# A 31-tap depthwise convolution as block-Toeplitz products, in the mixer of a decoder layer

## The chip, the cores and the metric

The kernel runs on one core of a Trainium2 chip, in one launch. The metric is the time on the device in microseconds (us), the median of the runs. Engines: TensorE (PE), VectorE (DVE), ScalarE (ACT), GpSimd (POOL) and SyncE (SP), which only issues DMAs here. Each runs its own queue of instructions in order; they meet at semaphores.

## The reference

One decoder layer on 1024 prompt tokens and 8 x 4 sample tokens: FFN 1, a mixer, FFN 2, and a gated embedding. The change is in the mixer's convolution head:

```python
h = rmsnorm(x, pre_g)
u = h @ w_in
u_val, u_glu, u_x, u_gelu = jnp.split(u, [D_CONV, 2 * D_CONV, 2 * D_CONV + D_LRU], axis=-1)
g = u_val * jax.nn.sigmoid(u_glu)
gp = jnp.concatenate([conv_buf, g], axis=1)          # 30 past rows in front
c = causal_dwconv(gp, conv_w, conv_b)                # 31 taps, each channel by itself
c = jax.nn.silu(rmsnorm(c, conv_norm_g))
new_conv_buf = gp[:, -(CONV_WIDTH - 1):, :]
```

D_CONV is 512 channels. The prompt has zeros in front, the eight sample sequences have a cache of 30 rows each. Beside it stands the RG-LRU head on u_x (a 4-tap convolution, two gates, a linear recurrence over time); both heads go through w_out.

## The kernel before

Features lie on the partitions, tokens along the free axis: 1056 tokens in three chunks c of C = 352, of which the last has 320 prompt and 32 sample tokens. Most matrices are fp32 split into a high and a low part in a rounded format, and each product is three passes (L589 to L591). `tile_product` is 8 x 3 such products with 352 columns. Weights come in units of 256 columns through one raw buffer: SP loads two halves (`load_wide`), ACT rounds them (`split_half`), DVE takes the rest (`split_tile`). A down weight of an FFN comes the same way through `rawd`: `load_down`, `split_down`.

Each FFN has NI = 11 steps; in a step PE forms gate and up tiles, then down tiles. The first and the last step are written out, nine are in a loop. SP has a loop of its own (`ffn_loads`), and after it load_down and two load_wide for the last step and the mixer. In the last step (`ffn_last`) the norms of the earlier chunks are done beside the products.

In the mixer, `vg_chunk` and `in_unit(2)`, `in_unit(3)` form u_val and u_glu for the four channel groups j of 128; DVE scales them by the norm and multiplies by the sigmoid, into `gp` (prompt, with 30 columns of history) and `gs` (samples). Then come twelve turns x. In a turn PE does the tile of u_x for one j and c, `conv_group` for another j and c, and `lru_gates` (six products into ps_aux). DVE does `lru_front` (scale, four taps, low part, with ACT's rounding `xc_hi` between), five of its own conv taps, and `lru_scan` of the turn before. ACT does sigmoids, exp, tanh, square root, with a table load (1.28 us) at each switch. lru_r, lru_i, lru_a and lru_q exist once, so the gates of turn x wait for the scan of turn x - 1, and xc exists twice.

The 31 taps are shared out: TP = 15 are products with a diagonal matrix on PE (fp32, not split), 16 are multiply-adds over all tokens on DVE (`conv_taps`), and `conv_join` adds both. ACT writes the diagonals (`diagonals`). `conv_states` carries the last 30 columns back to token order by PE transposes, for the new caches. After the turns follow gelu (units 6 and 7), the convolution's norm and silu, and w_out.

PSUM has a ring of six banks whose order is worked out ahead (`ring_plan`), and two more banks, ps_aux, in an order of their own (`aux_plan`). Each engine's order is written by hand.

Of the kernel before, what the change touches and what calls it, by code (L numbers as in the profile page):

```python
# [21 lines left out]
F32 = mybir.dt.float32  # L22
# [4 lines left out]
P = 128  # L27
# [3 lines left out]
NJ = 4  # L31
# [9 lines left out]
TP = 15  # L41
# [21 lines left out]
def ring_plan():  # L63
# [21 lines left out]
    for s in range(2):  # L85
        put("cache", s)
    for u in (2, 3):
        for c in range(NC):
            for t in range(2):
                put("in", u, c, t)  # L90
    for x in range(NJ * NC):
        put("in", 4 + x // 6, x % 6 // 2, x % 2)
        put("conv", x // NC, x % NC)
        if x == 0:
            for s in range(3):
                put("convout", s)
# [41 lines left out]

def aux_plan():
# [9 lines left out]
    for i in range(first):  # L149
        norm(i)  # L150
    for x in range(4 * NC):
        for which in "ri":
            at[which, x] = n
            n += 1
# [37 lines left out]
def build(nc, a, out):  # L192
    ctx = ExitStack()
    with ctx:
# [60 lines left out]
        y_lo, yl_at, _ = place("y_lo", [P, KT, TOK], F32R)  # L255
        gp, g_at, _ = place("gp", [P, NJ, CH + SEQ])
        mix_end = at[0]

        gs, _, e = place("gs", [P, NJ, NB, CH + DEC], offset=norm_at)
        assert e <= sq_at  # L260
        assert max(ffn_end, mix_end) <= nc.sbuf_usable_end, (ffn_end, mix_end, nc.sbuf_usable_end)
        row = 4 * TOK
        conv = place("conv", [P, NJ, TOK], offset=yl_at)[0]
        hs = place("hs", [P, NJ, TOK], offset=yl_at + 4 * row)[0]
        cache_in = place("cache_in", [P, 2, NJ * P], offset=yl_at + 4 * row)[0]
        gs_new = place("gs_new", [P, NJ, NB * CH], offset=yl_at + 4 * row)[0]
        gate_raw = place("gate_raw", [P, 2, NJ, P], offset=yl_at + 4 * row + 4096)[0]
        cv_stage = place("cv_stage", [P, 3, NJ * P], offset=yl_at + 6 * row)[0]
# [4 lines left out]
        diag, _, e = place("diag", [P, TP, P], offset=e)  # L273
        assert e <= yh_at + 4 * row
        gw_hi, _, e = place("gw_hi", [P, 2, NJ, P], F32R, offset=yh_at + 4 * row)
        gw_lo, _, e = place("gw_lo", [P, 2, NJ, P], F32R, offset=e)
        assert e <= yh_at + 6 * row
        xc = place("xc", [P, 2, C], offset=yh_at + 6 * row)[0]
        lru_r = place("lru_r", [P, C], offset=yh_at + 6 * row + 8 * C)[0]
        lru_i = place("lru_i", [P, C], offset=yh_at + 6 * row + 12 * C)[0]  # L280
        lru_a = place("lru_a", [P, C], offset=yh_at + 6 * row + 16 * C)[0]
        lru_q = place("lru_q", [P, C], offset=yh_at + 6 * row + 20 * C)[0]
        glu = place("glu", [P, 2, C], offset=yl_at + 6 * row)[0]
# [4 lines left out]
        assert e <= mix_end  # L288

# [28 lines left out]
        def conv_w(tap, j):  # L318
            n = P + tap * NJ + j
            return params[:, n:n + 1]  # L320
# [37 lines left out]
        cache_read = sem("cache_read")  # L358
# [4 lines left out]
        gs_new_done = sem("gs_new_done")  # L363
        conv_step = sem("conv_step")
        diag_done = sem("diag_done")
        diag_free = sem("diag_free")
# [78 lines left out]
        def _(sp_eng):  # L445
# [18 lines left out]
            def ffn_loads(f):  # L464
# [38 lines left out]
            eng.wait_ge(psum_full, RING["ffn", 0] + NI * STEP)  # L503
            for s in range(2):
                eng.dma_start(cache_in[0:4 * CH, s, :],
                              a["cache_conv"][0, 4 * s:4 * s + 4].rearrange("b w n -> (b w) n")
                              ).then_inc(cache_read, 16)
# [15 lines left out]
            for v in range(WIDE0["mix"] + 6, WIDE0["mix"] + 9):  # L523
                load_wide(v)
# [1717 lines left out]
```

## Time and profile before

| | us |
|---|---|
| median of 3 runs | 2345.52 |
| lowest, highest | 2345.4, 2349.55 |
| span of the profiled execution | 2337.7 |
| PE, DVE, ACT busy in it | 2158.0, 1317.6, 769.8 |

The span runs from the first to the last instruction; the runs' times hold in addition what lies around it, 7.8 us at the median. In rows of the profile, L589 is line 589 of the kernel, `out<-in` names tiles, `x24` counts instructions. In timelines the first column is the start, the second the length (of a merged row, from the first start to the last end); brackets give the idle time in front and who ended it. PE products overlap, so starts are compared, not lengths.

### The profile page before, as it was taken

To read this page: it belongs to the slowest core of one execution; us is meant where nothing else is said; L and a number is where in the kernel's file an instruction comes from. 1 tells how busy PE (TensorE), PEld (TensorE's weight loads), DVE (VectorE), ACT (ScalarE), POOL (GpSimd) and SP (SyncE) were. 2 spreads that over 40 slices of the span, in tenths; PEclk is the share of its full clock that TensorE was granted. 3 is DMA by queue.
4 is the path that set the end of the run, shared out by engine and by line. 5 is a ranking of instruction groups with operands and counts; after the bars stand their busy time and mean duration, and the time that the engine had idled before them with its cause. 6 is when DMAs were issued, how large, how long until landed. Compare 5 with 4: busy or idle time off the path is not lost. (4 is left out here: it accounts for less than half of the span.)

```text
span 2337.7 us, 34611 instructions
## 1 busy us (share of the span) xinstructions
PE 2158.0 (92%) x13020; PEld 2106.1 (90%) x13020; DVE 1317.6 (56%) x2620; ACT 769.8 (33%) x1500; POOL 0.9 (0%) x8
## 2 busy tenths in 40 slices
PE   5899999999999878999989689999999999995886
PEld 5899999999999878887789689999999999995886
DVE  4544444543445666988555764545434554557686
ACT  4311121221122333365575532212221121225563
POOL 0000000000000000000000000000000000000000
PEclk8999999999999889999999889999999999998897
DMA  4101111101111011100014201111101111102222
GB/s 149 37 28 45 54 54 54 54 27 35 45 54 54 1 45 41 46 1 19 19 38 144 91 1 55 55 54 54 45 18 45 54 54 54 54 1 73 72 91 75
DMA packets 92360, 116.15 MB, mean 50 GB/s; under 512 B 4596, under 2 KB 83704, under 8 KB 92282
## 3 DMA queue, kind: packets, MB, share of 16 engines
q1 hardware_dynamic: 91065, 110.79, 14.4%
q10 hardware_dynamic: 1216, 4.33, 0.6%
q8 instruction: 48, 0.79, 0.1%
q14 instruction: 31, 0.25, 0.0%
HBM read 110.15 MB, written 4.95 MB: 49 GB/s over the span
## 5 line engine op out<-in xcount | busy, mean ns | idle before, releaser
L589 PE MATMUL ps<-x_hi,w_lo 128*128 128x352 f32 x2688 | 883.2, 329 | 17.8 <-DVE w_lo L1503 8.8
L590 PE MATMUL ps<-x_lo,w_hi 128*128 128x352 f32 x2688 | 872.9, 325 | 0.0
L591 PE MATMUL ps<-x_hi,w_hi 128*128 128x352 f32 x2688 | 871.9, 324 | 0.0
L589 PEld LDWEIGHTS ps<-x_hi,w_lo 128*128 128x128 f32 x2688 | 514.6, 191 | 19.1 <-DVE w_lo L1503 9.5
L590 PEld LDWEIGHTS ps<-x_lo,w_hi 128*128 128x128 f32 x2688 | 515.3, 192 | 0.0
L591 PEld LDWEIGHTS ps<-x_hi,w_hi 128*128 128x128 f32 x2688 | 513.5, 191 | 0.0
L589 PE MATMUL ps<-a_hi,wd_lo 128*128 128x352 f32 x1104 | 361.6, 328 | 24.6 <-DVE a_lo L1600 11.6
L590 PE MATMUL ps<-a_lo,wd_hi 128*128 128x352 f32 x1104 | 357.7, 324 | 0.0
L591 PE MATMUL ps<-a_hi,wd_hi 128*128 128x352 f32 x1104 | 357.3, 324 | 0.0
L1650 DVE TENSOR_TENSOR acc<-ps,acc 128x352 f32<-128x352 f32 x480 | 249.3, 523 | 88.7 <-PE ps L591 82.8
L1583 DVE TENSOR_TENSOR tmp_u<-ps,rstd_pre 128x352 f32<-128x352 f32 x132 | 69.1, 524 | 370.7 <-PE ps L591 370.7
L1022 ACT ACTIVATE w_hi<-raw,params 128x256 fp32r<-128x256 f32 x512 | 213.6, 496 | 132.0 <-DMA raw<-in_ffn_w_gu_dram 109.1
L1503 DVE SCALAR_TENSOR_TENSOR w_lo<-raw,params,w_hi 128x256 fp32r<-128x256 f32 x512 | 225.8, 477 | 46.7 <-ACT w_hi L1022 46.7
L1089 ACT ACTIVATE tmp_s<-tmp_g 128x352 f32<-128x352 f32 x132 | 65.3, 498 | 552.1 <-DVE tmp_g L1583 552.1
L589 PEld LDWEIGHTS ps<-a_hi,wd_lo 128*128 128x128 f32 x1104 | 210.4, 191 | 27.6 <-DVE a_lo L1600 12.8
L590 PEld LDWEIGHTS ps<-a_lo,wd_hi 128*128 128x128 f32 x1104 | 210.9, 191 | 0.0
L591 PEld LDWEIGHTS ps<-a_hi,wd_hi 128*128 128x128 f32 x1104 | 210.1, 190 | 0.0
L1583 DVE TENSOR_TENSOR tmp_g<-ps,rstd_pre 128x352 f32<-128x352 f32 x132 | 68.5, 522 | 244.1 <-PE ps L591 230.0
L1098 ACT ACTIVATE a_hi<-tmp_a 128x352 fp32r<-128x352 f32 x132 | 59.9, 494 | 418.4 <-DVE tmp_a L1594 418.4
L829 PE MATMUL ps<-gp,diag 128*128 128x352 f32 (+1 forms) x360 | 108.8, 460 | 3.5 <-ACT diag L1284 3.5
L1526 DVE TENSOR_TENSOR ssum<-ssum,sq 128x352 f32<-128x352 f32 x177 | 92.6, 523 | 22.3 <-ACT sq L1048 9.5
L829 PEld LDWEIGHTS ps<-gp,diag 128*128 128x128 f32 x360 | 69.2, 194 | 38.1 <-issue 5.5
(172 smaller groups left out, 1678.2 us busy)
## 6 DMA issues: line engine op xcount, KB each, us to landing
raw<-in_ffn_w_gu_dram SPq DMA_DIRECT2D x88, 512.0 KB, 3.5
rawd<-in_ffn_w_down_dram SPq DMA_DIRECT2D x22, 1024.0 KB, 7.6
raw<-in_w_out_dram SPq DMA_DIRECT2D x24, 512.0 KB, 3.5
raw<-in_ple_w_gate_dram SPq DMA_DIRECT2D x24, 512.0 KB, 3.4
raw<-in_w_in_dram SPq DMA_DIRECT2D x16, 512.0 KB, 4.0
x_in<-in_x_prompt_dram ACTq DMA_DIRECT2D x6, 512.0 KB, 7.8
out_dram<-y_stage SPq DMA_DIRECT2D x6, 512.0 KB, 2.8
rawd<-in_ple_w_proj_dram SPq DMA_DIRECT2D x1, 1024.0 KB, 7.2
```

Source lines behind the costliest of these rows:

```text
L589: eng.matmul(dst, wl, xh, start=first, stop=False)
L590: eng.matmul(dst, wh, xl, start=False, stop=False)
L591: return eng.matmul(dst, wh, xh, start=False, stop=last)
L829: mm = eng.matmul(dst[:, 0:w], diag[:, tap, :], gp[:, j, at0:at0 + w], start=tap == 0, stop=tap == TP - 1)
L1022: ins = eng.activation(w_hi[s][:, sl], raw[:, sl], ACT.Copy, scale=vec(gain, k))
L1089: eng.activation(tmp_s[:, h, :], tmp_g[:, h, :], ACT.Silu).then_inc(silu_done, 1)
L1098: eng.activation(a_hi[:, h, cols(c)], tmp_a[:, h, :], ACT.Copy).then_inc(a_hi_done, 1)
L1503: ins = eng.scalar_tensor_tensor(w_lo[s][:, sl], raw[:, sl], vec(gain, k), f32(w_hi[s][:, sl]), ALU.mult, ALU.subtract)
L1526: eng.tensor_tensor(ssum[:, i % 2, :], ssum[:, i % 2, :], sq[:, (ADD0[i] + m - 1) % SQ, :], ALU.add).then_inc(add_done, 1)
L1583: eng.tensor_tensor((tmp_u if up else tmp_g)[:, h, :], src, rstd_pre[:, cols(c)], ALU.mult).then_inc(psum_free, 1)
L1650: eng.tensor_tensor(acc[:, m, cols(c)], src, acc[:, m, cols(c)], ALU.add).then_inc(psum_free, 1)
```

## The change

The convolution is written as products along time. Time is cut in blocks of BLK = 32. DVE transposes each 32x32 square of `gsrc` (channels x time, j odd and even in turn) into `gt_even` or `gt_odd`, so that a partition is a place in the block and each of four groups of 32 partitions holds 32 channels of its own. For one channel in each of the four groups at once (`cc`), a 128x128 matrix with four Toeplitz squares on its diagonal acts on 48 block columns (32 of the prompt, 16 for the samples); a second matrix does so on the block before. `conv_slot(t)` is that for CG = 8 values of cc: 16 full fp32 products. Sixteen slots t make up the four j. ACT copies a slot to `zt` (`conv_evict`), DVE transposes back (`to_channels`), and the bias is added later, inside the square and the scale.

The Toeplitz squares come from a table in DRAM. DVE lays the reversed taps in `rev` after step 0 of FFN 1; SP writes shifted rows of it to `toeplitz`, eight DMAs behind its loop in FFN 1; each slot loads its part with four DMAs (`load_toep`), alternately into two buffers. GpSimd clears the buffers and carries caches in and new caches out straight from gt. The twelve turns lose conv_group, conv_taps, conv_join and the diagonals; slots 0 to 7 stand between the tiles of units 2 and 3, slots 8 to 15 in turns 1 to 4.

```diff
+def conv_after(x):
+    return range(2 * CSLOT + 2 * (x - 1), 2 * CSLOT + 2 * x) if 1 <= x <= CSLOT else ()
...
+                if f == 0:
+                    eng.wait_ge(rev_done, 2)
+                    for j in range(NJ):
+                        for half in range(2):
+                            first = rev[:, j, 2 * BLK * half + BLK - 1:2 * BLK * half + BLK]
+                            rows = bass.AP(tensor=first.tensor, offset=first.offset,
+                                           ap=[first.ap[0], [-1, BLK], [1, BLK]])
+                            eng.dma_start(toep_dram[P * j:P * j + P, half, :, :], rows
+                                          ).then_inc(taps_out, 16)
                 load_down(d0 + NI - 1, down_src[f][NI - 1])
...
+            def load_toep(t):
+                if t < 2:
+                    eng.wait_ge(taps_out, 16 * 2 * NJ)
+                    eng.wait_ge(zero_done, (7, 5)[t])
+                else:
+                    eng.wait_ge(aux_full, AUX["conv", t - 2] + 1)
+                if t == 2 * CSLOT + 1:
+                    eng.wait_ge(zero_done, 8)
+                j, s = divmod(t, CSLOT)
+                for q in range(4):
+                    src = toep_dram[P * j + BLK * q + CG * s:P * j + BLK * q + CG * s + CG
+                                    ].rearrange("c h p n -> p (c h) n")
+                    eng.dma_start(toep(t)[BLK * q:BLK * q + BLK, :, :, BLK * q:BLK * q + BLK
+                                          ].rearrange("p cc b n -> p (cc b) n"), src
+                                  ).then_inc(toep_in[t % 2], 16)
...
+            def conv_slot(t):
+                j, s = divmod(t, CSLOT)
+                n = AUX["conv", t]
+                eng.wait_ge(aux_free, n - 1)
+                if s == 0:
+                    eng.wait_ge(gt_done, 2 * j + 2)
+                    eng.wait_ge(cache_in[j % 2], 64 * (j // 2 + 1))
+                eng.wait_ge(toep_in[t % 2], 64 * (t // 2 + 1))
+                for cc in range(CG):
+                    dst = ps_aux[:, n % 2, cc * NOUT:cc * NOUT + NOUT]
+                    for back in range(2):
+                        mm = eng.matmul(dst, toep(t)[:, cc, back, :],
+                                        gt(j)[:, 1 - back:1 - back + NOUT, CG * s + cc],
+                                        start=back == 0, stop=back == 1)
+                mm.then_inc(aux_full, 1)
+
+            in_unit(2, lambda k: k >= 2 and conv_slot(k - 2))
+            in_unit(3, lambda k: k < CSLOT and conv_slot(CSLOT + k))
...
-                conv_group(x // NC, x % NC)
+                for slot in conv_after(x):
+                    conv_slot(slot)
                 if x == 0:
-                    conv_states()
                     eng.wait_ge(gw_lo_done, 1)
                 lru_gates(x)
...
                         if c == 1 and at == "g1":
                             root(post, 0)
+                            if f == 0:
+                                eng.wait_ge(taps_out, 16 * 2 * NJ)
                             spread(post, 0)
...
+            def to_blocks(j):
+                eng.wait_ge(glu_done, 6 * (j // 2 + 1))
+                if j < 2:
+                    eng.wait_ge(zero_done, 5)
+                else:
+                    eng.wait_ge(aux_full, AUX["conv", CSLOT * (j - 2) + CSLOT - 1] + 1)
+                    eng.wait_ge(conv_out, 16 * 12 * (j - 1))
+                eng.transpose(gt(j)[:, 2 * NB + 1:, :],
+                              gsrc[:, j % 2, 0:SEQ].rearrange("p (n t) -> p n t", t=BLK)
+                              ).then_inc(gt_done, 1)
+                eng.transpose(gt(j)[:, 1:2 * NB:2, :],
+                              gsrc[:, j % 2, SEQ:].rearrange("p (n t) -> p n t", t=BLK)
+                              ).then_inc(gt_done, 1)
...
             for x in range(12):
                 lru_front(x)
-                if x:
-                    lru_one_minus(x - 1)
-                conv_taps(5)
                 if x == 0:
-                    conv_join(0, 0)
-                    conv_states()
                     continue
+                lru_one_minus(x - 1)
+                if x == 3:
+                    to_channels(2)
                 lru_scan(x - 1)
-                conv_join(x // NC, x % NC)
                 if x == 5:
+                    to_channels(3)
                     split_wide(WIDE0["mix"] + 6)
```

The order of instructions at three places. SP, from its loop in FFN 1 into the mixer, before:

```order
L462 DMA rawd<-in_ffn_w_down_dram 128x2x1024
L455 DMA raw<-in_w_in_dram 128x4x256 x4
L505 DMA cache_in<-in_cache_conv_dram 120x512 x2
L455 DMA raw<-in_w_in_dram 128x4x256 x2
L513 DMA gate_raw<-in_lru_wa_dram 64x4x64 x2
L513 DMA gate_raw<-in_lru_wx_dram 64x4x64 x2
L455 DMA raw<-in_w_in_dram 128x4x256 x6
```

and after (toep_mid and toep_first are the two buffers of slots 1 and 0):

```order
L496 DMA toeplitz<-rev 128x32x32 [waits rev_done]
L496 DMA toeplitz<-rev 128x32x32 x7
L478 DMA rawd<-in_ffn_w_down_dram 128x2x1024 [waits down_lo]
L471 DMA raw<-in_w_in_dram 128x4x256 [waits wide_lo] x6
L551 DMA gate_raw<-in_lru_wa_dram 64x4x64 [waits gate_zero]
L551 DMA gate_raw<-in_lru_wa_dram 64x4x64
L551 DMA gate_raw<-in_lru_wx_dram 64x4x64 x2
L542 DMA toep_mid<-toeplitz 32x16x32 [waits zero_done,taps_out]
L542 DMA toep_mid<-toeplitz 32x16x32 x3
L471 DMA raw<-in_w_in_dram 128x4x256 [waits wide_lo] x2
L542 DMA toep_first<-toeplitz 32x16x32 [waits zero_done,taps_out]
L542 DMA toep_first<-toeplitz 32x16x32 x3
```

The eight table DMAs stand in front of the last down weight, and the Toeplitz loads of slots 1 and 0 behind the gate weights.

PE, at the end of the tile of turn 1 and into its gates, before:

```order
L591 MATMUL ps<-x_hi,w_hi_51 128x352
L829 MATMUL ps<-gp,diag 128x352 x15
L589 MATMUL ps_aux<-xc_hi,gw_lo 128x352
L590 MATMUL ps_aux<-xc_lo,gw_hi 128x352
L591 MATMUL ps_aux<-xc_hi,gw_hi 128x352
```

and after:

```order
L677 MATMUL ps<-x_hi,w_hi_51 128x352
L906 MATMUL ps_aux<-gt_even,toep_first 128x48 x16
L906 MATMUL ps_aux<-gt_even,toep_end 128x48 x16
L675 MATMUL ps_aux<-xc_hi,gw_lo 128x352
L676 MATMUL ps_aux<-xc_lo,gw_hi 128x352
L677 MATMUL ps_aux<-xc_hi,gw_hi 128x352
```

Two slots take the place of the group in turns 1 to 4; in the turns 0 and 5 to 11 nothing does.

DVE, from the last glu product of unit 3 to the front of turn 0, before (gs_new is a copy for the new caches):

```order
L1812 TENSOR_TENSOR gp<-gp,glu 128x320 [waits sig_done,psum_free]
L1815 TENSOR_TENSOR gs<-gs,glu 128x8x4
L1503 SCALAR_TENSOR_TENSOR w_lo_54<-raw,params,w_hi_52 128x256 [waits wide_hi]
L1503 SCALAR_TENSOR_TENSOR w_lo_54<-raw,params,w_hi_52 128x256 x3
L1503 SCALAR_TENSOR_TENSOR w_lo_54<-raw,params,w_hi_52 128x256 [waits wide_hi]
L1503 SCALAR_TENSOR_TENSOR w_lo_54<-raw,params,w_hi_52 128x256 x3
L1922 COPY gs_new<-gs 128x960 [waits glu_done]
L1932 MEMSET ux_p 128x3
```

and after:

```order
L1903 TENSOR_TENSOR gsrc<-gsrc,glu 128x8x4
L1960 STREAM_TRANSPOSE zs<-zt 128x256 [waits aux_free]
L1961 STREAM_TRANSPOSE conv<-zt 128x1024 [waits dve_own]
L1963 COPY conv<-zs 128x32
L1949 STREAM_TRANSPOSE gt_even<-gsrc 128x1024 [waits conv_out,aux_full,glu_done]
L1952 STREAM_TRANSPOSE gt_even<-gsrc 128x8x32
L1949 STREAM_TRANSPOSE gt_odd<-gsrc 128x1024 [waits conv_out,aux_full,glu_done]
L1952 STREAM_TRANSPOSE gt_odd<-gsrc 128x8x32
L1577 SCALAR_TENSOR_TENSOR w_lo_54<-raw,params,w_hi_52 128x256 [waits wide_hi]
```

Six transposes now stand between the last glu product and the weight split that the front of turn 0 follows.

## Rows read from the trace of the kernel before

**Rows 1.** The page, part 1: busy time, share of the span, instructions.

```profile
PE 2158.0 (92%) x13020; PEld 2106.1 (90%) x13020; DVE 1317.6 (56%) x2620; ACT 769.8 (33%) x1500; POOL 0.9 (0%) x8
```

**Rows 2.** Busy time by stretch: units 2 and 3, then the twelve turns.

```profile
core 0: us, PE busy (x) PEld busy (x) DVE busy (x) ACT busy (x) POOL busy (x), PEclk, DMA share, GB/s
912.80:958.80 46.00, 46.00 (x289) 46.00 (x290) 38.65 (x79) 10.61 (x23) 0.00 (x0) 1.00 0.24 75
958.80:1146.90 188.10, 180.89 (x854) 143.53 (x853) 153.26 (x327) 107.40 (x189) 0.00 (x0) 0.97 0.05 15
```

**Rows 3.** Timeline of PE, turns 0 to 2.

```profile
977.73 0.41 PE L589 MATMUL ps_aux<-xc_hi,gw_lo 128*128 128x352 f32 x1
...
978.77 0.32 PE L589 MATMUL ps<-x_hi,w_lo 128*128 128x352 f32 x1
...
982.63 9.04 PE L829 MATMUL ps<-gp,diag 128*128 128x352 f32 x30
991.24 0.59 PE L589 MATMUL ps_aux<-xc_hi,gw_lo 128*128 128x352 f32 x1
...
996.30 3.43 PE L823 MATMUL ps<-gs,diag 128*128 128x32 f32 x30
999.56 1.83 PE L829 MATMUL ps<-gp,diag 128*128 128x320 f32 x3
```

**Rows 4.** DVE by line and shape, 912 to 1150 us: busy, mean ns.

```profile
L1886 DVE SCALAR_TENSOR_TENSOR conv<-gp,params,conv 128x1024 f32<-128x1024 f32 x60 | 76.4, 1274 | 0.0
L1886 DVE SCALAR_TENSOR_TENSOR conv<-gs,params,conv 128x32 f32<-128x32 f32 x60 | 14.5, 241 | 0.0
```

**Rows 5.** Timelines of DVE and ACT, the front of a turn.

```profile
1014.46 0.53 DVE L1941 TENSOR_TENSOR ux_p<-ps,rstd_pre 128x352 f32<-128x352 f32 x1 [4.17 <-issue]
1015.02 0.46 DVE L1962 TENSOR_SCALAR xc<-ux_p,params 128x352 f32<-128x352 f32 x1
1015.52 1.83 DVE L1965 SCALAR_TENSOR_TENSOR xc<-ux_p,params,xc 128x352 f32<-128x352 f32 x3
1017.91 0.53 DVE L1975 TENSOR_TENSOR xc_lo<-xc,xc_hi 128x352 fp32r<-128x352 f32 x1 [0.56 <-ACT xc_hi L1251]
...
1017.38 0.50 ACT L1251 ACTIVATE xc_hi<-xc 128x352 fp32r<-128x352 f32 x1 [2.05 <-DVE xc L1965]
```

**Rows 6.** Timelines of SP, ACT, DVE and PE, last step of FFN 1.

```profile
727.73 0.38 SPq L462 DMA_DIRECT2D rawd<-in_ffn_w_down_dram  x1
...
747.91 1.90 ACT L1033 ACTIVATE wd_hi<-rawd 128x2048 fp32r<-128x2048 f32 x1
...
749.84 2.29 DVE L1518 TENSOR_TENSOR wd_lo<-rawd,wd_hi 128x2048 fp32r<-128x2048 f32 x1 [2.37 <-ACT wd_hi L1033]
...
760.97 0.63 PE L589 MATMUL ps<-a_hi,wd_lo 128*128 128x352 f32 x1 [2.62 <-issue]
```

**Rows 7.** DMA: 915.5 to 919.5 (256-byte packets), 1000 to 1100 (1 KB), landing of rawd.

```profile
DMA packets 816, 0.20 MB, mean 49 GB/s; under 512 B 816, under 2 KB 816, under 8 KB 816
## 3 DMA queue, kind: packets, MB, share of 16 engines
q1 hardware_dynamic: 816, 0.20, 21.7%
...
q1 hardware_dynamic: 1056, 1.05, 3.3%
...
DMA to landing us min/median/max: 5.6/6.9/8.2
```

**Rows 8.** PE after waits in the tail, and its clock by stretch (fourth number).

```profile
1166.29 0.86 PE L628 MATMUL ps_aux<-ones,ssum 128*128 128x1 f32 x6 [4.12 <-DVE ssum L1526]
...
1195.69 1.60 PE L640 MATMUL ps_aux<-ident,std 128*128 128x128 f32 x6 [5.77 <-DVE std L1541]
...
1168.00:1170.00 2.00, 2.00 (x8) 0.50 0.00 0
1170.00:1172.00 2.00, 2.00 (x13) 0.91 0.00 0
...
1200.00:1202.00 2.00, 2.00 (x11) 0.73 0.00 0
1000.00:1001.00 1.00, 1.00 (x3) 0.50 0.00 0
...
1091.00:1094.00 3.00, 3.00 (x29) 1.00 0.00 0
```

More of the change, by code:

```diff
@@ L84, in ring_plan @@
             put("vg", c, t)
-    for s in range(2):
-        put("cache", s)
-    for u in (2, 3):
+    for u in (2, 3, 4, 5):
         for c in range(NC):
@@ L150, in aux_plan @@
         norm(i)
+    for t in range(2 * CSLOT):
+        at["conv", t] = n
+        n += 1
     for x in range(4 * NC):
+        for t in conv_after(x):
+            at["conv", t] = n
+            n += 1
         for which in "ri":
@@ L357, in build @@
         glu_done = sem("glu_done")
-        cache_read = sem("cache_read")
+        rev_done = sem("rev_done")
+        taps_out = sem("taps_out")
+        zero_done = sem("zero_done")
+        cache_in = [sem(f"cache_in{b}") for b in range(2)]
+        toep_in = [sem(f"toep_in{b}") for b in range(2)]
+        gt_done = sem("gt_done")
+        conv_back = sem("conv_back")
         gate_in = sem("gate_in")
@@ L1240, in _, with conv_evict @@
             split_wide(WIDE0["mix"] + 3)
+            def conv_evict(t):
+                j, s = divmod(t, CSLOT)
+                n = AUX["conv", t]
+                eng.wait_ge(aux_full, n + 1)
+                if s == 0 and j:
+                    eng.wait_ge(conv_back, 2 * j)
+                src = ps_aux[:, n % 2, 0:CG * NOUT].rearrange("p (cc m) -> p m cc", cc=CG)
+                eng.activation(zt[:, 0:SEQ // BLK, CG * s:CG * s + CG], src[:, 2 * NB:NOUT, :],
+                               ACT.Copy)
+                eng.activation(zt[:, SEQ // BLK:, CG * s:CG * s + CG], src[:, 0:2 * NB:2, :],
+                               ACT.Copy).then_inc(aux_free, 1)
+            for t in range(CSLOT):
+                conv_evict(t)
             split_wide(WIDE0["mix"] + 4)
@@ L1275, in lru_root @@
                 eng.activation(lru_q[:, :], lru_q[:, :], ACT.Sqrt).then_inc(lru_sqrt, 1)
-            def diagonals(j):
-                for tap in range(TP):
-                    if j and tap < TP - 1:
-                        eng.wait_ge(diag_free, (TP - 1) * (j - 1) + tap + 1)
-                    elif j:
-                        eng.wait_ge(psum_full, RING["conv", j - 1, 2] + 1)
-                    eng.activation(diag[:, tap, :], ident[:, :], ACT.Copy, scale=conv_w(tap, j)
-                                   ).then_inc(diag_done, 1)
-            diagonals(0)
             for x in range(12):
@@ L1291, in _ @@
                     lru_root(x - 1)
-                if x % 3 == 2 and x < 11:
-                    diagonals(x // 3 + 1)
+                for t in conv_after(x):
+                    conv_evict(t)
                 lru_gates(x)
@@ L1729, in vectors, with reverse_taps @@
                                            None, ALU.mult))
+            def reverse_taps():
+                done(eng.memset(rev[:, :, :], 0.0))
+                taps = params[:, P:P + CW * NJ].rearrange("p (t j) -> p j t", j=NJ)
+                eng.tensor_copy(rev[:, :, BLK - 1:BLK - 1 + CW], taps[:, :, ::-1]
+                                ).then_inc(rev_done, 1)
+                eng.tensor_copy(rev[:, :, 2 * BLK:2 * BLK + CW - 1], taps[:, :, CW - 2::-1]
+                                ).then_inc(rev_done, 1)
             def softplus():
@@ L1771, in _ @@
             softplus()
+            reverse_taps()
             with eng.Fori(1, NI - 1) as i:
```

269 lines of the change are left out of this document (120 added, 149 removed).

## The prediction

> **What bounds the kernel now.** I read the page first: TensorE (PE) is busy for 92% of the span [rows 1], so work taken off another engine counts only where PE waits for it. Then the busy time by stretch [rows 2]. The convolution lives in two stretches of the mixer. From 912.8 to 958.8 us PE forms input units 2 and 3 and never pauses. From 958.8 to 1146.9, twelve turns of tile, convolution group and recurrence gates, it is busy 180.9 of 188.1 us, while VectorE (DVE) has 153 and ScalarE (ACT) 107. So PE sets the time there, although DVE holds 64 taps of 1.5 us [rows 4]. The last view is the timeline of one turn [rows 3]: a tile takes 982.63 - 978.77 = 3.86 us, a convolution group 991.24 - 982.63 = 8.61, the six gate products about 1.0. A group of the third chunk starts with 15 products of 32 columns, 999.56 - 996.30 = 3.26 us, and then 15 of 320 columns (7.8, scaled from 8.61).
>
> **Removed.** PE: 8 x 8.61 + 4 x (3.26 + 7.8) = 113 us of diagonal products, and the state transposes (1 us). DVE: 64 taps, of which 60 take 1.27 + 0.24 us [rows 4], some 90 us, and the joins. ACT: 60 diagonals. The DVE and ACT parts were beside PE and are worth nothing by themselves.
>
> **Added on PE: 16 slots.** A slot is 16 full fp32 products of 48 columns, each with weights of its own. Each fp32 product is two records. In [rows 3] the 30 records with 32 columns take 109 ns each although their columns are few, so the weights set the pace, and a slot costs 32 x 109 ns = 3.5 us, 56 us for 16. Lower end the same (nothing in the trace has weights loaded faster). The moving operand is read with a stride of 32 elements, which no row shows; the upper end is 7.0, the same slot at the low clock.
>
> **Units 2 and 3: +33 us.** Eight slots stand between these tiles: +28. Slot 0 also waits: PE is there at 912.8 + 3 x 3.86 = 924.4. SP can start on its Toeplitz loads only when the four gate loads are issued (918.7), then issues four DMAs of 0.64, two weight halves, and four more, until 924.8. With the queued weights in front I have them landed at 929.2: +4.9. Later loads follow the slot two before and have 10 us for 2.6 of issue and 2.4 of landing; I cost them at nothing while a slot's 2048 pieces of 128 bytes take under 5 us. Unit 3 ends at 991.8 instead of 958.8.
>
> **Turn 0: -5 us.** Before, 958.8 to 978.8. Now nothing of the convolution stands before gates(0), but DVE must first do glu and sigmoid (1.6), to_channels(1) (2.0), to_blocks(2) and (3) (3.2), what is left of the weight split (3.2) and the front, with gates 5.2 in all: 15.2 us. Of the DVE transposes no row exists; I take 1.27 us for 1024 elements, as the tap on the same shape [rows 4]. Down to 0.8 or up to double, it moves the turn by -2 to +4.
>
> **Turns 1 to 4: 47 us.** Two slots in each: 4 x (3.86 + 7.0 + 1.0) = 47.4, PE-bound.
>
> **Turns 5 to 11: 74 us, and no longer PE-bound.** PE gives tile x only after gates(x - 1), and gates(x) need the DVE front of tile x. Before, a convolution group lay under that front. Now it is a loop: 0.25 to start, 1018.44 - 1014.46 = 4.0 for scale, four taps, ACT's rounding and the low part [rows 5], 0.1, gates 1.0 and tile 3.86, together 9.2 us. Chunk 2 adds some 0.6 (small pieces like the 0.24 in [rows 4]). Turn 6 also carries to_channels(3) and a weight split, with ACT and DVE in series: 17. Sum 9.8 + 17 + 3 x 9.2 + 2 x 9.8 = 74. Gates(11) end at 991.8 + 15.2 + 47.4 + 74 = 1128.4, 18.5 earlier than 1146.9. Behind them scan(10) is now late by 3 us, where it used to be finished early, and that costs the tail some 1.9. Left: -16.6 us, at full clock.
>
> **The clock: +18 us.** PE now waits nine times for over 4 us: before slot 0, before gates(0), and in each of turns 5 to 11. The two waits of such length in the next stage show what follows [rows 8]: after 4.12 us PE runs at 0.50 of full clock (1.2 GHz) until about 1170.4, that is 4.1 us; after 5.77 us from 1195.7 to 1201.1, 5.4 us. That loses 2.0 and 2.7. I take 2.0 for each of nine (a turn has only 4.9 us of products, so it can't lose much more). The lower end is nothing, since a wait of 2.62 us before 760.97 [rows 6] is cheap; the upper is 9 x 2.7 = 24. The Trainium skill, TensorE: Matmul & The Clock Gate, section HAM oscillation, says that a kernel that waits between bursts pays for warming up at each burst; the trace agrees with 2.0 to 2.7 us for each of the two. Left: +1.4.
>
> **The tap table: +15 us, the largest doubt.** Before the last step of FFN 1, SP now issues eight DMAs that write rev to DRAM: 8 x 4096 = 32768 pieces of 128 bytes, 2048 for each of 16 engines. Behind them in the same queue stands the last down weight rawd, before issued at 727.7 and used by ACT from 747.9 [rows 6]. Behind a late rawd stand ACT's copy (1.9), DVE's split (2.3) and scale, product and low part (3.5), 7.7 us, until PE may start the down products, before at 760.97. With the shortest landing of rawd, 5.6 [rows 7], PE is delayed by 727.7 + X + 5.6 + 7.7 - 761.0 = X - 20, where X is what the taps hold the queue for. Price of a packet: 1 KB 3.3% x 100 x 16 / 1056 = 50 ns; 256 bytes 21.7% x 4 x 16 / 816 = 17 ns [rows 7]. By the nearest row X = 2048 x 17 ns = 35 us: +15. By the line through both, 11.5 ns, X = 24: +4. If a piece costs as much as 1 KB, X = 102: +82. I take 17 ns, since these are stores to DRAM and no row has such small ones. The stall lies in front of everything else and nothing later takes it back. The Trainium skill, DMA: Bandwidth & Descriptors, section Why small descriptors are slow, has a fixed overhead of about 3 cycles per packet, 11 cycles for 256 bytes; at its 850 MHz that is 13 ns where the trace has 17, and an estimate from it for 128 bytes is 8 ns, X = 17, no stall, and a sum of about 2347.
>
> **Costed at nothing.** reverse_taps (DVE, after FFN step 0, waits for nobody in a stage that PE bounds). The evictions (ACT, two small activations per slot for five 128x128 diagonals per turn). GpSimd's 48 state stores and 16 cache loads: it was idle, but to_blocks(3) waits for the first 24 stores, which leaves some 1.8 us for each; its DMAs have no row, SP's take 0.25 to 0.8 to issue. If they took 3.5, to_blocks(3) and all behind it would be about 29 late. The new wait of ACT for taps_out, before spread of post1 at 783, would stop its norm and behind it all squares; it is met unless X exceeds 50.
>
> **The sum.** The profiled execution has a span of 2337.7, the median of the runs is 2345.5; I add differences to the latter. 2345.5 - 16.6 + 18 + 15 = 2361.9, say 2362.
>
> **Rivals.**
> - *Tap table covered, clock as above*: X is 20 or less; the page's price is this case. 2345.5 + 1.4 = 2347. For it: 1 KB packets are dearer only by their bytes. Chance 0.15.
> - *The faster end*: the clock holds. PE's short waits in turns 5 to 11 don't bring it down (only two long waits, 4 us in all), and X stays near the line, 24 or less (+2). PE then sheds 57 us of products and gives back 40 to the new loop: 2345.5 - 16.6 + 4 + 2 = 2335, and 2331 with faster transposes. Against it: both waits over 4 us in [rows 8] were followed by 0.50. It decides at waits in which the clock survives 4.3 us. Chance 0.17.
> - *The slots bring the clock down*: one of the four bursts of 32 columns (996.3) was followed by 0.50, another kept 1.00 [rows 8]. Two slots in a row last 7 us. Then the second takes 7.0 instead of 3.5 and the tile behind it loses 2: 4 x 5.5 = +22, 2384. Chance 0.20.
> - *Small pieces are dear*: 30 ns each make X = 61, +41, and the Toeplitz loads or GpSimd's queue may become late as well: 2388 and more. Chance 0.10.
> - The forecast itself, 2350 to 2376: 0.38.
>
> **How the numbers follow.** Range 2334 to 2400: it leaves out nearly half of the faster case, the far part of the dear pieces, and a tail of the slots' case, under 0.2 together. 0.2% is 4.7 us, about what a measurement can tell from no change. Faster than 2341: the second rival and a little of the first, 0.19. Within: most of the first, 0.14. Slower: 0.67.
>
> **What would show it.** Right: a PE idle stretch before the last down products of FFN 1 that ends after 770, with SP's rawd landing late; slots of 3.5 us; turns 5 to 11 near 9.2 us plus the clock's 2, with DVE's ux_p released by PE and PE's gates by xc_lo; DVE busy far below 153 us and worth nothing; PEclk between 0.5 and 1 there. Wrong: a rawd that lands before 753 (tap table free), slots much over 3.5 us at full clock (strided reads), turns 1 to 4 that wait for Toeplitz loads, DVE transposes over 2.5 us, or gates(11) before 1130.

## The result, and the profile after

The changed kernel takes 2369.7 us (median of 4 runs, 2364.74 to 2374.89) against 2345.46 (2343.04 to 2349.55): a ratio of 1.0112 on record, with a 95% interval of 1.009 to 1.0134 (the two medians alone give 1.0103). By the medians that is 24 us more; the forecast was 2362, 16.5 more. The profiled execution has a span of 2369.0 us. The spans of the four runs are 2362.7 to 2372.8, so it is one of the longer ones; before it was 2337.7. A few of the 31 us between these two spans are therefore not the change's.

In the rows of after, L675 to L677 are the three passes of a product (L589 to L591 before), L906 is a slot. The page, part 1 and the clock of its part 2; in [rows 1] PE was busy 2158.0:

```profile
PE 2137.2 (90%) x13032; PEld 2120.5 (90%) x13032; DVE 1237.4 (52%) x2491; ACT 759.7 (32%) x1472; POOL 45.5 (2%) x79
...
PEclk7999999999999988977889889999999999998897
```

PE and DVE both lost work (21 and 80 us), and the time grew. PE lost little because it ran its work at a lower clock: 0.935 over the whole span, 0.959 before. Busy time by stretch, the answer to [rows 2]: units 2 and 3 with slots 0 to 7, turn 0, turns 1 to 4 with two slots each, turns 5 to 11. The columns are PE, PEld, DVE, ACT and POOL busy, granted clock, DMA share, GB/s.

```profile
917.70:1004.70 87.00, 82.50 (x545) 82.24 (x546) 23.31 (x50) 14.97 (x40) 18.96 (x32) 0.90 0.36 73
1004.70:1020.30 15.60, 5.83 (x31) 5.58 (x30) 12.21 (x28) 4.75 (x11) 9.02 (x14) 0.71 0.38 87
1020.30:1086.10 65.80, 65.80 (x378) 65.68 (x377) 25.05 (x54) 32.17 (x55) 6.98 (x12) 0.71 0.18 29
1086.10:1171.60 85.50, 48.45 (x211) 46.43 (x211) 48.47 (x130) 55.04 (x79) 0.00 (x0) 0.78 0.04 13
```

The third line is where the time went beyond the forecast: PE is busy all the 65.8 us, but at a granted clock of 0.71, between its two levels of 1.2 and 2.4 GHz (0.50 and 1.00). The fourth shows PE idle for 37 of 85.5 us, about as forecast. Gates(11) end at 1171.6, 24.7 later than 1146.9.

The timelines of SP, ACT and PE at the last step of FFN 1 answer to [rows 6]:

```profile
727.42 23.05 SPq L496 DMA_DIRECT2D toeplitz<-rev  x8
750.51 3.06 SPq L478 DMA_DIRECT2D rawd<-in_ffn_w_down_dram  x1
...
758.63 1.91 ACT L1096 ACTIVATE wd_hi<-rawd 128x2048 fp32r<-128x2048 f32 x1 [10.94 <-DMA rawd<-in_ffn_w_down_dram]
...
766.22 0.63 PE L675 MATMUL ps<-a_hi,wd_lo 128*128 128x352 f32 x1 [8.18 <-issue]
```

The eight tap DMAs hold SP for 23 us. Before, rawd had landed 5.6 us after its issue, by 733.3, and ACT copied it at 747.9; now ACT waits for it until 758.6, and PE waits 8.18 us where it waited 2.62.

The clock of PE around slots, by stretch: a single slot in units 2 and 3 and the start of the tile behind the next one; then the first slot of turn 1, its second, gates with the start of the tile, and the rest of it:

```profile
945.80:949.40 3.60, 3.60 (x34) 3.60 (x33) 0.52 (x1) 0.00 (x0) 0.00 (x0) 1.00 0.01 2
...
956.70:958.70 2.00, 2.00 (x9) 2.00 (x8) 0.00 (x0) 0.50 (x2) 0.00 (x0) 0.52 0.34 53
...
1024.80:1028.00 3.20, 3.20 (x31) 3.20 (x30) 2.74 (x5) 0.13 (x1) 2.48 (x5) 1.00 0.15 21
1028.00:1034.80 6.80, 6.80 (x36) 6.80 (x35) 2.87 (x6) 2.53 (x5) 0.00 (x0) 0.53 0.25 39
1034.90:1038.50 3.60, 3.60 (x13) 3.57 (x14) 0.00 (x0) 2.78 (x5) 0.00 (x0) 0.50 0.47 73
1038.50:1041.40 2.90, 2.90 (x19) 2.90 (x19) 0.00 (x0) 2.85 (x4) 0.00 (x0) 0.97 0.02 6
```

Two slots in a row begin at full clock and end at half. In turns 1 to 4 the second takes 5.7 to 6.6 us, the gates 1.9 instead of 1.0, and each tile 4.4 to 5.3 instead of 3.9. One slot between two tiles mostly leaves the clock where it was, though twice in units 2 and 3 the tile behind it started at half (956.7 here, and 980.4).

The waits of PE in the timeline of slot 0, gates(0), gates(5), gates(6) and gates(7), where [rows 8] had shown two such waits in the stage behind:

```profile
933.92 7.03 PE L906 MATMUL ps_aux<-gt_even,toep_first 128*128 128x48 f32 x32 [4.50 <-DMA toep_first<-toeplitz]
...
1018.43 0.63 PE L675 MATMUL ps_aux<-xc_hi,gw_lo 128*128 128x352 f32 x1 [9.77 <-issue]
...
1096.65 0.64 PE L675 MATMUL ps_aux<-xc_hi,gw_lo 128*128 128x352 f32 x1 [4.83 <-DVE xc_lo L2039]
...
1113.52 0.66 PE L675 MATMUL ps_aux<-xc_hi,gw_lo 128*128 128x352 f32 x1 [10.23 <-DVE xc_lo L2039]
...
1124.32 0.66 PE L675 MATMUL ps_aux<-xc_hi,gw_lo 128*128 128x352 f32 x1 [4.07 <-DVE xc_lo L2039]
```

The new small operations, grouped by line and shape, 905 to 1190 us (busy, mean ns):

```profile
L1961 DVE STREAM_TRANSPOSE conv<-zt 128x1024 f32<-128x1024 f32 x4 | 5.0, 1246 | 0.1
L1952 DVE STREAM_TRANSPOSE gt_even<-gsrc 128x256 f32<-128x256 f32 x2 | 0.8, 398 | 0.0
L632 POOL DMA_DIRECT2D out_dram<-gt_even x8 | 5.1, 637 | 0.0
L1316 ACT ACTIVATE zt<-ps_aux 128x256 f32<-128x256 f32 x16 | 6.1, 381 | 55.0 <-PE ps_aux L906 54.0 <-DVE conv L1963 1.0
```

### The profile page after: what moved, and what is told of

The parts are those of the page before. It is cut to its first block and busy times, and to the rows that moved or that the text cites. A ratio compares the mean times of both kernels' runs of the same rounds, so it can differ in the third digit from the quotient of the medians.

```text
span 2369.0 us, 34627 instructions
## 1 busy us (share of the span) xinstructions
PE 2137.2 (90%) x13032; PEld 2120.5 (90%) x13032; DVE 1237.4 (52%) x2491; ACT 759.7 (32%) x1472; POOL 45.5 (2%) x79
## 3 DMA queue, kind: packets, MB, share of 16 engines
q0 software_dynamic: 2048, 1.06, 0.3%
## 5 line engine op out<-in xcount | busy, mean ns | idle before, releaser
L675 PE MATMUL ps<-x_hi,w_lo 128*128 128x352 f32 x2688 | 892.6, 332 | 18.7 <-DVE w_lo L1577 9.5
L677 PE MATMUL ps<-x_hi,w_hi 128*128 128x352 f32 x2688 | 880.1, 327 | 0.0
L675 PEld LDWEIGHTS ps<-x_hi,w_lo 128*128 128x128 f32 x2688 | 522.6, 194 | 20.0 <-DVE w_lo L1577 10.2
L676 PEld LDWEIGHTS ps<-x_lo,w_hi 128*128 128x128 f32 x2688 | 522.6, 194 | 0.0
L677 PEld LDWEIGHTS ps<-x_hi,w_hi 128*128 128x128 f32 x2688 | 520.7, 194 | 0.0
L675 PE MATMUL ps<-a_hi,wd_lo 128*128 128x352 f32 x1104 | 361.7, 328 | 30.3 <-issue 12.3
L677 PE MATMUL ps<-a_hi,wd_hi 128*128 128x352 f32 x1104 | 357.5, 324 | 0.0
L675 PEld LDWEIGHTS ps<-a_hi,wd_lo 128*128 128x128 f32 x1104 | 210.6, 191 | 33.2 <-issue 12.9
L677 PEld LDWEIGHTS ps<-a_hi,wd_hi 128*128 128x128 f32 x1104 | 210.2, 190 | 0.0
L714 PEld LDWEIGHTS ps_aux<-ones,ssum 128*128 128x128 f32 x162 | 27.3, 246 | 75.5 <-DVE ssum L1600 75.4
L714 PE MATMUL ps_aux<-ones,ssum 128*128 128x1 f32 x162 | 27.5, 285 | 72.7 <-DVE ssum L1600 72.7
```

The costliest lines, as they stand in the source:

```text
L675: eng.matmul(dst, wl, xh, start=first, stop=False)
L676: eng.matmul(dst, wh, xl, start=False, stop=False)
L677: return eng.matmul(dst, wh, xh, start=False, stop=last)
L714: mm = eng.matmul(ps_aux[:, n % 2, q:q + 1], ssum[:, i % 2, t0:t0 + P], ones[:, 0:1], start=True, stop=True)
```

## The experiments

All are compared by their ratio to the kernel before, timed in the same session; its median there was 2342 to 2344. The changed kernel stands at 1.0112, which on that scale is 2368 (2366 by the ratio of the medians). Where the text gives a turn, it is the distance between the starts of two gates.

### The tap table behind rawd, and twice

```diff
+                load_down(d0 + NI - 1, down_src[f][NI - 1])
                 if f == 0:
                     eng.wait_ge(rev_done, 2)
...
-                load_down(d0 + NI - 1, down_src[f][NI - 1])
```

> The eight tap-table DMAs stand behind the last rawd instead of in front of it. Theory (the taps delay rawd, and rawd delays the down products): the PE wait before the last down products of FFN 1 is back to 2.6 us and ends near 761 instead of 766.2, every later mark of the changed kernel moves 5 us forward, and the time is 2369.7 - 5 = 2365. Rival (PE is late there for the 32768 small pieces on the DMA engines, wherever they stand in the queue, or the two wide weight loads behind them become late for the mixer): the gain is given back before 917, and the time stays at 2368 to 2372.

Measured: 2360.4 us, ratio 1.0085 (1.0068 to 1.0102). The timeline of PE at the same place:

```profile
756.39 0.40 PE L675 MATMUL ps<-a_hi,wd_lo 128*128 128x352 f32 x1 [2.62 <-issue]
```

The wait is back to 2.62, a gain of 5.56 us, and nothing gives it back. The start itself moved by 9.8, since this execution had also run the steps before somewhat faster (its rawd was issued 4.3 us earlier); so the wait, not the start, prices the term. The clock behind the wait differed as well. In the kernel before it stood at half behind the same wait of 2.62 us, and here at full. The first line is before, the second this run:

```profile
761.00:764.00 3.00, 3.00 (x10) 3.00 (x11) 0.53 (x1) 0.34 (x1) 0.00 (x0) 0.50 0.02 5
...
756.40:759.40 3.00, 3.00 (x19) 3.00 (x20) 1.05 (x2) 0.73 (x2) 0.00 (x0) 1.00 0.10 32
```

The four tiles behind it took 16.95 us before, 16.70 in the changed kernel and 15.50 here. So one wait can go with either clock, and no run tells what decided it. The other way round, the table is written twice, the second time into a spare one:

```diff
-                    for j in range(NJ):
+                    for copy, j in [(n, j) for n in range(2) for j in range(NJ)]:
```

> The eight tap-table DMAs are issued twice, the second time into a spare table, all ahead of the last rawd. Theory (X is linear in the pieces, 2048 pieces in 23 us on each engine, 11 us per thousand): SP issues rawd at 774 instead of 750.5, the PE wait before the last down products of FFN 1 is 31 us instead of 8.2, and the time is 2370 + 23 = 2393. Rival (the first eight were slow for another reason, for instance the wide weight loads that share the engines, and a further piece is cheaper, some 8 ns): X grows by 16, the wait is 24, 2386.

```profile
727.14 22.92 SPq L497 DMA_DIRECT2D toeplitz<-rev  x8
750.11 24.49 SPq L497 DMA_DIRECT2D toep_spare<-rev  x8
774.64 2.97 SPq L479 DMA_DIRECT2D rawd<-in_ffn_w_down_dram  x1
...
790.24 0.63 PE L676 MATMUL ps<-a_hi,wd_lo 128*128 128x352 f32 x1 [32.48 <-issue]
```

The wait grows by 24.3 us. The piece of 128 bytes costs 23.05 / 2048 = 11.3 ns in the changed kernel and 12.0 in the second table here: nearly linear. The single run took 2399.6 us, 31 to 34 above the changed kernel on this scale, where 23 was expected. The wait is 24.3 of it, 2.4 more had come up by the start of unit 2, and the rest is not explained.

### Slot 0 one tile later

```diff
-            in_unit(2, lambda k: k >= 2 and conv_slot(k - 2))
-            in_unit(3, lambda k: k < CSLOT and conv_slot(CSLOT + k))
+            in_unit(2, lambda k: k >= 3 and conv_slot(k - 3))
+            in_unit(3, lambda k: k <= CSLOT and conv_slot(CSLOT - 1 + k))
```

> Slots 0 to 7 each stand one tile later in units 2 and 3; nothing else is moved. Theory (slot 0 waits for the Toeplitz loads, and that wait brings the clock down): the wait of 4.5 us is gone, slot 0 takes 3.7 instead of 7.0 and the tile behind it 3.9 instead of 5.2, so unit 3 ends 9 us earlier against its start, and the time is 2361. Rival (the slot brings the clock down, not the wait): only the 4.5 us are gained, 2365.

Measured: 2361.8, ratio 1.0088 (1.0068 to 1.0107). Slot 0 still waits 1.7 us and takes 5.4; from the first tile of unit 2 to gates(0) it is 93.6 us instead of 100.8. Of the 7.2 us gained, 2.8 are the wait (4.5 to 1.7) and 1.4 slot 0 itself. The rest lies in the two later tiles that had started at half clock and here did not. That doesn't come from the edit: the kernels with the tap table behind rawd and with the spread slots have units 2 and 3 of the changed kernel, and in their profiles no later tile was slow either. So the wait cost its own length and a clock fall in slot 0, as the theory has it, but the edit took only part of it away. In the last kernel below slot 0 has no wait and takes 3.5 us; the tile behind it still took 5.5.

### The slots spread over turns 0 to 6

```diff
-    return range(2 * CSLOT + 2 * (x - 1), 2 * CSLOT + 2 * x) if 1 <= x <= CSLOT else ()
+    first = 2 * CSLOT
+    if x == 0:
+        return range(first, first + 1)
+    if x == 1:
+        return range(first + 1, first + 3)
+    return range(first + 1 + x, first + 2 + x) if x <= 6 else ()
```

> The last eight slots go to turns 0 (one), 1 (two) and 2 to 6 (one each), instead of two in each of turns 1 to 4; to_channels(3) moves from turn 5 to turn 7. Theory (two slots in a row bring the clock down, one alone doesn't, and one hides under the front of a turn): slots of 3.5 us, tile 3.9, gates 1.0, turns 2 to 5 near 10.5 us each and turn 6 near 14, so the stretch from gates(0) to gates(6) shrinks from 95 to some 70 us, and the time is about 2345. Rival (every slot brings the clock down, alone as well, in a stretch where the tile is single too): slot 7.0, tile 5.2, gates 2.1, turns of 14.3, the stretch is 90 us and the time 2365.

Measured: 2358.4, ratio 1.0079 (1.0059 to 1.0098). Gates(0) to gates(6) take 84.4 us instead of 95.1: between the two theories. The timeline of PE in turn 2 (here L911 is the slot, L680 to L682 the passes):

```profile
1039.66 3.69 PE L911 MATMUL ps_aux<-gt_even,toep_end 128*128 128x48 f32 x32
1043.95 0.66 PE L680 MATMUL ps_aux<-xc_hi,gw_lo 128*128 128x352 f32 x1 [0.60 <-DVE xc_lo L2044]
...
1046.63 0.49 PE L680 MATMUL ps<-x_hi,w_lo 128*128 128x352 f32 x1
```

The slot alone runs at full clock; the gates run at half and the tile behind them starts at half (granted 0.50 until 1049.0). It isn't the pair alone, then: slot, short waits and gates in a row are enough.

### The tile ahead of the gates

```diff
+            tile(0)
+            for x in range(NJ * NC):
                 for slot in conv_after(x):
                     conv_slot(slot)
+                if x < 11:
+                    tile(x + 1)
```

> PE forms tile x + 1 before the gates of turn x, in all twelve turns; nothing else is moved. Theory (turns 5 to 11 are a loop through tile, front and gates, which this opens; what is left is ACT's chain of sigmoid, exp, tanh, square, root and DVE's scan, some 8.5 us): turns 7 to 11 take 8.5 to 9.3 us instead of 10.6 to 12.0, the wait before gates(0) falls from 9.8 to 5.9, turns 1 to 4 stay at 16.4 since PE bounds them, and the time is about 2348. Rival (the loop through ACT and DVE's scan is as long as the other, so that opening one changes nothing): turns 7 to 11 stay at 11, only turn 0 gains, 2366.

Measured: 2360.8, ratio 1.0084 (1.0067 to 1.0101). Turns 7 to 11 take 7.7 to 9.0 us, better than the theory said, and gates(6) to gates(11) 40.0 instead of 56.2. The stretch of the last three of them by engine:

```profile
1142.80:1166.10 23.30, 13.85 (x67) 12.82 (x67) 18.62 (x48) 21.99 (x31) 0.00 (x0) 0.75 0.00 0
```

ACT is busy 22.0 of 23.3 us: the loop through tile and front is gone and ACT, with its three table loads of 1.28 us in each turn, is the bound. But gates(0) to gates(4) grew from 65.8 to 80.3, which neither theory had. There the two slots now stood right behind the gates, in turns 2 to 4 with a wait of 1.5 us for ACT to read the gates' bank, and took 11 to 14 us at low clock.

### Slot, tile, slot

> As the kernel with tile x + 1 ahead of the gates, but in turns 1 to 4 the order is slot, tile x + 1, slot, gates x instead of slot, slot, tile x + 1, gates x. Theory (the clock falls when low-work stretches follow each other: slots, gates and short waits; a tile between them holds it, as in units 2 and 3, where the tile behind a single slot mostly ran at 1.00): slots 3.5 and tile 3.9, turns 1 to 4 take some 12.5 us each instead of 20 with the tile ahead, the stretch from gates(0) to gates(4) is 50 us instead of 80, and the time is 2361 - 30 = 2331. Rival (the density of the whole turn decides, two slots for each tile are too thin in any order): slots and tile at 0.5 most of the time, 17 to 20 us a turn, 2350 to 2360.

```diff
+                slots = list(conv_after(x))
+                if x and slots:
+                    conv_slot(slots.pop(0))
+                if x < 11:
+                    tile(x + 1)
+                for slot in slots:
                     conv_slot(slot)
```

Measured: 2349.2, ratio 1.0028 (1.0011 to 1.0045). Gates(0) to gates(4) take 67.4 us, 16.8 a turn, where the theory said 12.5 and the rival 17 to 20. A tile between the slots helps (80 to 67) and doesn't hold the clock.

### Thin slots

> The eight slots of turns 1 to 4 form one channel instead of eight (2 products instead of 16), so most of the convolution of j = 2 and 3 is left out; all waits, loads and evictions stay. Theory (these slots cost their own time and hold the clock down for gates and tile): turns 1 to 4 become loops like turns 7 to 9, 10.6 us each instead of 16.4, so the stretch from gates(0) to gates(4) is 43 us instead of 66, and the time 2347. Rival (the turns are bound by Toeplitz loads or ACT's evictions, not by PE): they stay above 14 us, 2362 or more.

```diff
-                for cc in range(CG):
+                for cc in range(CG if t < 2 * CSLOT else 1):
```

This kernel leaves out most of the convolution of j = 2 and 3. One run of 2355.3 us. Gates(0) to gates(4) take 54.3 us, not 43 and not 56 or more. PE now waits 5 to 6 us in each of these turns:

```profile
1031.65 0.63 PE L675 MATMUL ps_aux<-xc_hi,gw_lo 128*128 128x352 f32 x1 [4.95 <-ACT zt L1318]
```

What ends the wait is ACT's eviction of the slot, and not xc_lo as in the later turns: on ACT it stands behind xc_hi, a table load of 1.28 us and the square root. So the turns become loops of 13.6 us through tile, front and eviction, and the rival named the right wait, but with full slots it doesn't bound the turns: there PE never waits. Taking away nearly all the work of eight slots, some 36 us of PE, bought 11.5: with the slots the turn is bound by PE, and without them the loop stands just behind.

### All together, and the place of the tile

The combined kernel has the tap table behind rawd, slots 0 to 7 one tile later, the spread slots, and the tile ahead, in the order slot, tile, gates.

> All at once: the tap table behind the last rawd (-5), slots 0 to 7 one tile later (-7), slots 8 to 15 in turns 0 (one), 1 (two) and 2 to 6 (one each), tile x + 1 ahead of the gates, with the tile between the two slots of turn 1. Theory (clock holds where a tile stands between slots): turns 1 to 6 are PE-bound at 8.5 us (12 for turn 1), turn 6 has the weight split in addition, turns 7 to 11 are 7.8, the stretch from gates(0) to gates(11) is 105 us instead of 151, and the time is 2370 - 5 - 7 - 46 = 2312, faster than the kernel before. Rival (one slot for each tile still brings the clock down when gates and waits join it): turns 2 to 6 at 12 to 14 us, 2340.

Measured: 2333.7, ratio 0.996 (0.9943 to 0.9978): faster than both. But gates(0) to gates(11) take 129 us instead of the 105 expected, with 13.3 to 13.4 for each of turns 2 to 5. In the next kernel only the order within a turn differs (tile, slot, gates):

> As the combined kernel, but in turns 1 to 6 tile x + 1 stands ahead of the slots of the turn instead of between or behind them (tile, slot, gates, tile, slot, gates). Theory (in the combined kernel the slot right behind the gates waits 1.5 us for ACT to read the gates' bank, and that wait with gates and slot brings the clock down, so that the tile takes 5.2 to 6.4; with the tile between there is no wait): slot 3.5, tile 3.9, gates 1.0, turns 2 to 6 take 8.5 us instead of 13.3, turn 1 some 14, gates(0) to gates(6) take 58 us instead of 88, and the time is 2334 - 28 = 2306. Rival (the share of thin products in the turn decides, gates and slot together are over half of it, wherever the tile stands): the clock stays at 0.5 for most of each turn, 11 to 12.5 us a turn, 2325.

```diff
-                slots = list(conv_after(x))
-                if x and slots:
-                    conv_slot(slots.pop(0))
                 if x < 11:
                     tile(x + 1)
-                for slot in slots:
+                for slot in conv_after(x):
                     conv_slot(slot)
```

Measured: 2315.5, ratio 0.9875 (0.9836 to 0.9913). Turns 3 to 5 take 8.7 to 8.9 us. This took away the wait of 1.5 us behind the gates and also moved the slot from them. To tell the two apart, the same kernel got a wait of that kind in front of the tile:

```diff
+                if 2 <= x <= 6:
+                    eng.wait_ge(aux_free, AUX["r", x - 1] + 1)
```

> The kernel with tile, slot, gates, plus one wait: in turns 2 to 6 PE waits, before tile x + 1, until ACT has read the first gate bank of turn x - 1, which is the wait that the slot had in the combined kernel (1.5 us). It tells whether that wait or the place of the tile held the clock down there. Theory wait: the clock falls again, turns 2 to 5 take 12 us or more at a granted clock near 0.75, gates(1) to gates(5) take 48 us instead of 37, 2328. Theory place: the tile right behind the wait keeps the clock, each turn is only 1.5 us longer (10.3), gates(1) to gates(5) take 43 us, 2321.

Measured: 2320.3, ratio 0.9886 (0.9858 to 0.9915). PE now waits 1.17 us in these turns; gates(1) to gates(5) take 43.2 us, where the theory of the place said 43 and the other 48. Turns 3 to 5 by stretch, of the combined kernel:

```profile
1037.30:1077.20 39.90, 35.38 (x188) 34.52 (x187) 21.46 (x59) 23.15 (x36) 0.00 (x0) 0.74 0.09 14
```

with the tile in front:

```profile
1036.20:1062.50 26.30, 25.89 (x188) 25.01 (x188) 18.82 (x48) 23.39 (x36) 0.00 (x0) 1.00 0.20 32
```

and with the tile in front and the wait:

```profile
1036.50:1066.90 30.40, 26.70 (x189) 24.96 (x188) 18.20 (x49) 23.39 (x36) 0.00 (x0) 1.00 0.17 28
```

The same 188 records take 35.4 us of PE in the first and some 26 in the other two. In these turns a slot behind gates and a wait ends at half clock; a full tile behind the same gates and a wait of the same kind keeps the clock, and so does the slot behind it. It doesn't always: in turn 6 of the last of these traces the tile stands behind the same wait, and its clock is below full:

```profile
1069.60:1074.90 5.30, 5.30 (x24) 5.30 (x25) 0.39 (x1) 5.24 (x11) 0.00 (x0) 0.71 0.00 0
```

So the order accounts for the difference in turns 3 to 5, and the rule behind it is open.

### Fronts and table loads first

On top of that order, the first two Toeplitz loads stand ahead of the gate loads on SP (slots 0 to 7 are back at their old places), DVE does the front of turn 0 ahead of the weight split of unit 5, and its part of the split of unit 6 one turn later. Two later Toeplitz loads also move ahead of the weights of unit 6 on SP.

> As the kernel with tile, slot, gates; in addition the first two Toeplitz loads stand ahead of the gate loads on SP, slots 0 to 7 at the places of the changed kernel again, DVE forms the front of turn 0 ahead of the weight split of unit 5, and DVE's part of the weight split of unit 6 comes one turn later. Theory: slot 0 has no wait at its old place and takes 3.7, so units 2 and 3 take 78 to 80 us; gates(0) come 3.2 us earlier; the wait before gates(6) or (7) shrinks by some 3; in sum 6 to 9 us below the other kernel of this pair. Rival (slot 0 waits for to_blocks or for the gate's low share of the DMA queues, or what is moved on DVE is late one turn later): within 3 us of it.

```diff
             load_wide(WIDE0["mix"] + 2)
+            load_toep(1)
+            load_toep(0)
             eng.wait_ge(gate_zero, 1)
...
             to_blocks(3)
-            split_wide(WIDE0["mix"] + 5)
...
                 if x == 0:
+                    split_wide(WIDE0["mix"] + 5)
                     continue
...
-                if x == 5:
+                if x == 6:
                     split_wide(WIDE0["mix"] + 6)
```

Measured: 2301.4, ratio 0.9816 (0.9777 to 0.9854), 42 us below the kernel before and 14 below the kernel it starts from, more than the 6 to 9 expected. From the start of unit 2 to gates(0) it gains 7.1 us, in turn 1 3.2 and in turns 2 to 6 4.7, and turns 7 to 11 give back 2.3. Which of the four moves did what was not taken apart. Units 2 and 3 (first line) have no idle time, and unit 3 ends 78.0 us after the start of unit 2; most of turns 2 to 6 lies in the second:

```profile
912.00:994.00 82.00, 82.00 (x570) 82.00 (x571) 26.58 (x57) 18.28 (x49) 18.97 (x32) 0.96 0.32 72
...
1016.00:1060.00 44.00, 43.55 (x305) 42.38 (x304) 27.05 (x72) 38.33 (x61) 0.00 (x0) 0.96 0.15 24
```

From the start of unit 2 to gates(11) it takes 193.4 us, against 252.0 in the changed kernel. The kernel before with the same reorderings was not run; its PE idled only 7.2 us in the twelve turns [rows 2], so little is to be had there.

## Why the prediction was right or wrong

The direction and its main reason held, and 2370 lies within the range. The sum came near in part by luck: two errors of opposite sign, -10 us in the tap table and +18 in turns 1 to 4. Stage by stage, with the forecast's clock term put where its waits were:

| | forecast | measured |
|---|---|---|
| tap table | +15 | +5.2 |
| units 2 and 3 (from 46.0) | 81.0 | 87.0 |
| turn 0 (from 20.0) | 17.2 | 15.6 |
| turns 1 to 4 | 47.4 | 65.8 |
| turns 5 to 11 | 88 | 85.5 |
| gates(11) end | 1161.4 | 1171.6 |

**The tap table.** The mechanism was right: SP's queue, rawd, ACT's copy, 7.6 us to the down products (7.7 said), and the two kernels with the table behind rawd and written twice bear it out. The price was wrong. I took 17 ns a piece from the nearest row; measured is 11.3, which is the line through both rows of [rows 7] (11.5), so X is 22.8 and not 35. On the other side rawd took 8.1 us from issue to ACT's copy and not 5.6. X - 20 with these values gives 5.2. From the Trainium skill, DMA: Bandwidth & Descriptors, section Why small descriptors are slow, I had worked out an estimate of 8 ns and no stall; the piece cost 11.3 ns, and the stall was there, so here the measurement decides against both that estimate and my choice.

**Units 2 and 3.** A slot took 3.5 us between starts (945.76 to 949.25), so the strided reads cost nothing, and slot 0 waited 4.5 (4.9 said). What I missed is the clock: slot 0 took 6.8 and the tile behind it 1.1 us more (I had 2.0 for the wait in all), and two later tiles lost 1.6 each, with no wait in front of them. The run with early Toeplitz loads has 78.0 us there, though two of its tiles started at half clock too; without the wait of 4.9, my sum at full clock is 74.1, and the granted clock of 0.96 is the rest.

**Turn 0** held, and the transposes with it: 1.20 to 1.25 us for 1024 elements, 1.27 taken. The front began after the weight split, as worked out; in the last kernel, with that split behind the front, PE waits 0.27 us there instead of 2.37.

**Turns 1 to 4** are the step that failed: 3.86 + 7.0 + 1.0 at full clock. This was the third rival, *the slots bring the clock down*, with +22 us for these turns; the traces show +18.4 (65.8 - 47.4): 10.8 in the second slots, 4.0 in the tiles and 3.6 in the gates. My clock term stood only behind waits, and in these turns PE never waits. The rival had the place right, but not the cause: it is not the pair that does it. A single slot, followed by short waits and gates, did it too (turns of 10.8 to 14.3 us in the kernel with spread slots), and two slots with a tile between them still did. [rows 8] showed it for one of four bursts of 32 columns, and I gave it 0.20. The four bursts had long 320-column products right behind them, which the slots in turns 1 to 4 have not; that difference I should have weighed. What exactly brings the clock down stays open; the runs show in which orders it fell.

**Turns 5 to 11** held: a loop through the front of 9.2 us plus some 2 for the clock; turns 7 to 11 measured 10.6 to 12.0 and turn 6 16.9. Opening the loop took 16 us off gates(6) to gates(11), which shows it. All nine waits of over 4 us came. Behind six of the seven in these turns the gates ran at half clock, as forecast from two rows; gates(9), behind 4.12 us like its neighbours, took 1.09 us at full clock, and the fall came in the tile behind it. My lower end rested on a misread row: I called the wait of 2.62 us before 760.97 [rows 6] cheap, but the granted clock was 0.50 for 3 us behind it. On such waits the Trainium skill, TensorE: Matmul & The Clock Gate, section HAM oscillation, says that a kernel that waits between bursts pays at each one for warming up; the trace agrees, with gates at 1.9 us instead of 1.0 (but for gates(9)) and a tile of 4.6 to 5.9 instead of 3.9.

**Costed at nothing** held where it was checked: GpSimd's DMAs take 0.56 to 0.64 us each to issue (1.8 allowed), evictions 0.38 and 0.22, and no slot after slot 0 waited for its Toeplitz load. The tail lost 3.1 us (1.9 said): 1223.52 against 1195.69 is 27.8, of which 24.7 were there at gates(11). Of the other 3.5 us between the two profiled spans, which build up in FFN 2 and behind it, I have no cause; both kernels do the same work there.

## What to carry to other kernels

Products with few columns for each weight load are cheap only as long as the clock holds: try a dense tile right behind every wait, with the thin products behind that tile, and read the granted clock to see whether it holds. When a change frees the engine that bounds, look for the loop that its work had covered, and open it (here, form the next tile ahead of the gates) in the same edit. Count the pieces of a DMA, and put it behind the loads that something waits for.

## What the runs showed of the hardware

- The place of one 3.9 us tile went with the granted clock of turns 3 to 5: 0.74 with the thin products right behind gates and a wait, 1.00 with the tile there, waits of 1.2 us or not. In turn 6 the tile behind such a wait had 0.71.
- The same wait of 2.62 us was followed by a granted clock of 0.50 for 3 us in one kernel and of 1.00 in another.
- Full fp32 products of 48 columns that read their moving operand at a stride of 32 elements take 109 ns a record at full clock, as the 32-column ones did in [rows 3].
- A piece of 128 bytes to DRAM cost 11.3 to 12.0 ns on each of 16 DMA engines (the pieces shared out evenly), and SP was held as long: eight such issues took 23 us where the issue of a weight load took 0.4. Whether the engines or the issue set that pace was not tested.
- A DVE transpose in 32x32 squares of 128x1024 takes 1.20 to 1.25 us, of 128x256 0.40 to 0.44.
